# Second expert stage: the matrix engine's jump ahead of the first gather, seven zero products less

## What is computed

```python
probs_g = softmax(xf @ w_group + b_group);  p_top, g_idx = top_k(probs_g, 1)
in_group = (xf @ w_router + b_router) of group g_idx
w_top, e_local = top_k(softmax(in_group), 2);  w_top = w_top / sum(w_top)
gates = one_hot(g_idx * 4 + e_local) weighted by p_top * w_top
h = silu(einsum('td,edf->tef', xf, w_gate)) * einsum('td,edf->tef', xf, w_up)
y = einsum('tef,efd->td', h * gates[:, :, None], w_down)
```

## Time and profile before

| what | value |
|---|---|
| median of three runs (lowest, highest) | 907.32 us (905.35, 909.91) |
| profiled execution: span from first to last instruction | 902.7 us |
| PE busy in the span | 881.5 us (98%) |
| VectorE, ScalarE, GpSimd busy | 502.8, 391.4, 35.2 us |
| bytes moved, mean rate | 205.78 MB, 228 GB/s |

### The profile page before, as it was taken

One profiled execution on the slowest core, in us unless ns is written; L12 is line 12 of the kernel. 1 busy time (PEld: TensorE's weight loads), 2 busy tenths in 40 slices (PEclk: granted clock), 3 DMA queues, 4 the chain that ended last, 5 costly groups with the idle time before them and its releaser, 6 DMA issues.

```text
span 902.7 us, 13442 instructions
## 1 busy us (share of the span) xinstructions
PE 881.5 (98%) x5387; PEld 678.2 (75%) x5387; DVE 502.8 (56%) x752; ACT 391.4 (43%) x531; POOL 35.2 (4%) x73
## 2 busy tenths in 40 slices
PE   7999999989999999999999999999999999999998
PEld 6988998944543698878545446899877888888887
DVE  4798876711111965626211118465658777777576
ACT  4755654232221536551322215435545666655441
POOL 7100010000000000000000000000001000000010
PEclk9999999999999999999999999999999999999999
DMA  9934417979999574329599996354543655546611
GB/s 319 318 96 139 141 47 263 341 254 411 409 409 401 179 242 169 100 89 351 190 411 409 409 403 216 122 181 166 176 152 118 219 192 192 187 139 233 234 47 46
DMA packets 102828, 205.78 MB, mean 228 GB/s; under 512 B 6896, under 2 KB 57840, under 8 KB 102768
## 3 DMA queue, kind: packets, MB, share of 16 engines
q1 hardware_dynamic: 101184, 202.14, 62.6%
q10 hardware_dynamic: 1584, 2.81, 1.0%
HBM read 203.87 MB, written 1.05 MB: 227 GB/s over the span
## 4 chain that ended last, share of the span: by engine, by line
PE 83%; DVE 5%; DMA 5%; ACT 4%; issue 2%; SPq 1%; DVEq 0%; ACTq 0%
PE psum L709 80%; DVE w_lo L2116 2%; DMA raw<-in_w_kv_shared 2%; ACT w_hi L1639 1%; DMA raw<-in_attn_w_in 1%; DMA raw<-in_a_w_in 1%; ACT arena L1639 1%; SPq L361 1%; PE psum L817 1%; DMA x_res<-in_x 1%; ACT x_slots L1639 0%; PE psum L1504 0%; PE psum L922 0%; DVE xt L2137 0%; PE psum L1018 0%
## 5 line engine op out<-in xcount | busy, mean ns | idle before, releaser
L709 PE MATMUL psum<-xt,w_hi 128*128 128x256 f32 (+1 forms) x1056 | 253.8, 321 | 3.9 <-DVEq L2831 1.7
L2116 DVE TENSOR_TENSOR w_lo<-raw,w_hi 128x2048 fp32r<-128x2048 f32 x88 | 200.7, 2287 | 47.4 <-ACT w_hi L1639 44.3
L709 PE MATMUL psum<-xt,w_lo 128*128 128x256 f32 x704 | 198.2, 282 | 0.0
L709 PEld LDWEIGHTS psum<-xt,w_hi 128*128 128x128 f32 x1056 | 177.1, 190 | 19.4 <-issue 2.7
L1639 ACT ACTIVATE w_hi<-raw 128x2048 fp32r<-128x2048 f32 (+1 forms) x90 | 170.1, 1892 | 38.8 <-PE psum L709 23.4
L709 PEld LDWEIGHTS psum<-xt,w_lo 128*128 128x128 f32 x704 | 134.1, 191 | 0.0
L709 PE MATMUL psum<-w_hi,xt 128*128 128x512 f32 (+1 forms) x368 | 112.8, 379 | 0.0
L1639 ACT ACTIVATE arena<-psum 128x512 f32<-128x512 f32 (+2 forms) x70 | 40.8, 601 | 124.9 <-PE psum L709 82.6
L709 PE MATMUL psum<-hi_as_raw,x_slots 128*64 128x512 f32 x176 | 80.8, 596 | 0.0
L709 PE MATMUL psum<-lo_as_raw,x_slots 128*64 128x512 f32 x176 | 80.8, 596 | 0.0
L709 PEld LDWEIGHTS psum<-w_hi,xt 128*128 128x128 f32 x368 | 67.3, 189 | 12.6 <-DVE xt L2137 1.1
(11 more groups left out here) (267 smaller groups left out, 1245.0 us busy)
## 6 DMA issues: line engine op xcount, KB each, us to landing
hi_as_raw<-in_gate_up SPq DMA_DIRECT2D x44, 512.0 KB, 7.7
lo_as_raw<-in_gate_up SPq DMA_DIRECT2D x44, 512.0 KB, 9.1
raw<-in_ffn_w_up SPq DMA_DIRECT2D x44, 512.0 KB, 4.5
raw<-in_gate_up SPq DMA_DIRECT2D x40, 512.0 KB, 6.8
raw<-in_a_w_in SPq DMA_DIRECT2D x26, 512.0 KB, 7.5
raw<-in_w_down SPq DMA_DIRECT2D x24, 512.0 KB, 10.5
raw<-in_attn_w_in SPq DMA_DIRECT2D x24, 512.0 KB, 5.0
raw<-in_ffn_w_down SPq DMA_DIRECT2D x22, 512.0 KB, 4.1
```

Source lines behind the costliest of these rows:

```text
L709: return pe.matmul(o, l, r, start=start, stop=stop, skip_group_check=skip)
L2116: return dve.tensor_tensor(w_half(h, w_lo), w_half(h, raw), w_half(h, w_hi).bitcast(F32), ALU.subtract).then_inc(lo_split, 1)
```

## The change

In stage 2 the seven zero products behind the count go. The first gather becomes a function. In stage 1 (`layer == 0`) it is called where it stood, ahead of the jump; in stage 2 it is called as the first thing in each of the two arms, so that the jump stands directly behind the register load.

```diff
                     keep_busy(8, 7)
                     count_chosen()
-                    keep_busy(7, 7)
                 pe.wait_ge(sem("placed"), layer + 1)
                 load = pe.value_load(load_max[0:1, 0:1], min_val=0, max_val=T)
...
-                pe.wait_ge(s["perm_ready"], 1)
-                for b in range(TB):
-                    pe.wait_ge(sem("x_rest"), 2 * layer + b + 1)
-                    for r, bank in enumerate(FIRST_BANKS):
-                        gather_block(0, r, bank, b)
+                def first_gather():
+
+                    pe.wait_ge(s["perm_ready"], 1)
+                    for b in range(TB):
+                        pe.wait_ge(sem("x_rest"), 2 * layer + b + 1)
+                        for r, bank in enumerate(FIRST_BANKS):
+                            gather_block(0, r, bank, b)
+
+                if layer == 0:
+                    first_gather()
                 with pe.If(load > FAST_LIMIT):
+                    if layer:
+                        first_gather()
                     dense_path()
                 with pe.Else():
+                    if layer:
+                        first_gather()
                     short_path()
```

## The result

The changed kernel takes 909.91 us (median of 18 runs, 906.95 to 915.37); the kernel before, run beside it, 905.46 (18 runs, 902.65 to 910.52). The ratio is 1.0044, with a 95% interval of 1.0029 to 1.0059: **4.0 us slower** by the ratio (the two medians lie 4.45 apart), where 0.3 us gained was forecast. The profiled execution of the changed kernel spans 906.1 us and took 907.79.

The account below looks back on a forecast made before the run. PE was taken to bound the kernel; the jump's visible 1.59 us would vanish but return ahead of the gather, so expert products start at 435.5 instead of 435.8, 0.3 gained: 907.0 us from 907.32, range 905.0 to 910.0.

Parts of the forecast that it names:

- What bounds the kernel, and the two gaps: PE bounds the kernel; at stage 2's head only its gaps of 0.64 and 1.59 us can be taken back.
- The price of the jump, 3.35: From PE's branch to the arm's first product takes 3.35 us, 1.8 of it hidden behind the gather in stage 2.
- one price fits both stages: The 3.35 us from stage 1's gap of 3.10 also gives stage 2's arm start, 435.7 against 435.80 measured.
- The register load, 0.25: The load that the moved jump needs at once in stage 2 costs 0.25 us, with up to 4.3 possible.
- The code packet under load, +0: Fetching the arm's code during stage 2's DMA traffic adds nothing, with up to 0.5 us in the range.
- Rival C, the clock: PE's 3.8 us of idle time ahead of stage 2's gather lowers the clock: 1.6 to 3.5 us lost, chance 0.30.
- The zero products, 0.45 gained: Without the seven zero products in stage 2, PE's instruction stream goes on at 428.05 instead of 428.5, 0.45 us gained.
- The expert products: In stage 2 they follow the gather without a jump, at 435.5 instead of 435.8, with the gates in time.
- The range: 905.0 to 910.0 us for the changed kernel, with C's slow end, the long load and scatter outside, under 0.2.
- my -0.3: The forecast's sum at stage 2's head: expert products 0.3 us earlier, 907.0 for the median.

Follow-up runs that it names:

- e8: The kernel before with PE's two arms in the other order in both stages, the short arm next in the code: 911.16 us, ratio 1.0066.
- e9: The kernel before with prefetch hints for PE's jump of both expert stages, both ahead of the router's products: 903.28 us, ratio 0.9979.
- e11: The kernel before with prefetch hints for both jumps, stage 1's earlier, ahead of the second half of projection O0: 904.8 us, ratio 0.9990.
- e12: The kernel before with 12 zero products between the first gather and the jump, in both stages: 909.14 us, one time.
- e4: The changed kernel without stage 2's register load on PE, its jump asking the register of stage 1: 909.29 us, ratio 1.0039.
- e5: The kernel before once more, unchanged, for a second trace: 907.02 us, one time.
- e2: The kernel before without the seven zero products, the jump where it was: ratio 0.9999.
- e1: The changed kernel with the seven zero products back behind the count, so the jump's move alone: ratio 1.0056 of the kernel before.
- e6: The changed kernel with 24 zero products in stage 2 between the register load and the jump: 909.68 us, ratio 1.0050.
- e7: The changed kernel with PE's two arms in the other order in both stages, the short arm first: 917.94 us, ratio 1.0141.
- e10: The changed kernel with prefetch hints for both jumps, stage 1's ahead of the second half of projection O0: 904.72 us, 0.9995 of the kernel before.
- e3: The kernel before with the register load moved behind the gather, directly ahead of the jump, in both stages: ratio 1.0032, 2.9 us.

## Why the prediction was wrong

- **What bounds the kernel, and the two gaps**: right. The gap of 1.59 was the jump (e8, e9 and e11 take it away), and the jump comes back ahead of the gather.
- **The price of the jump, 3.35**: this is the step that failed. I let the stream follow the gather at 0.12 for each product, set the branch at its end, 180.95 and 432.35, and counted the price from there. In fact the stream is well ahead of the gather: the code packet comes at least 0.8 (changed kernel) and 1.9 us (e12) before the last weight load ahead of stage 1's jump. With nothing queued the price is 5.45 (e4), and the gather hid 3.4 to 3.9 of it (5.45 less the gaps of 2.07 and 1.59), not 1.8. Where the stream stands is known only roughly: from the gather's start to the expert products of stage 2 it is 5.65 in the first trace of before and 6.13 in e5, which at a price of 5.45 puts the jump 0.2 to 0.7 after that start, but 7.13 in e2, whose gather ran at the lower clock. Why it varies is open. That "one price fits both stages" was no test, because stage 1's 3.10 was that execution's (e5); the row that spoke against me stood in my own text, stage 2's packet 0.5 to 0.7 *before* the gather's last load, and I put it down to the wait for x. The Trainium skill (TensorE: Matmul & The Clock Gate, Architectural detail) gives TensorE's queue as 64 deep; the gather is 32 weight loads and 32 products, and e12 and the changed kernel's stage 1 agree with a stream that far ahead.
- **The register load, 0.25**: mis-sized, 1.4 (e4 against the changed kernel and e1, each one trace). It lay between my bounds, 0 and 4.3; I took the middle of 0 and 0.45, because both rows were of this very load. The 0 was no bound, since a stream that runs ahead passes the load while PE works on what is queued (stage 1's maximum is ready at 175.03, 2.2 before the gather). In e6 PE's first product behind the load starts 0.71 after M, so the load holds up the stream by no more than that, and the jump waits for the rest. Before, it ran beside the wait for x.
- **The code packet under load, +0**: open. I took stage 1's jump for one without traffic, but the 0.04 of the earlier trace rows begins at 181.2, and in the 3 us before it, where a stream that runs ahead meets the jump, the same trace has transfers (columns as in the earlier trace rows):

```profile
178.00:179.00 1.00, 1.00 (x10) 1.00 (x10) 0.43 (x3) 0.02 (x1) 0.00 (x0) 1.00 1.01 320
179.00:180.00 1.00, 1.00 (x11) 1.00 (x10) 0.00 (x0) 0.18 (x1) 0.00 (x0) 1.00 0.46 148
```

e4's 5.45 was measured under traffic too (share 1.04). No trace shows a far jump that was surely taken without transfers, so how much of the 5.45 is theirs is not shown.
- **Rival C, the clock**: right in kind, with its place ahead of the gather; 0.30 was too little, since the idle time came out at 7.13, not 3.8, and e2 shows a fall within 2.35. Its price, 5.51 - 4.05 = 1.5, is below my 1.9 to 3.8, since PE stood idle in the first half of the stretch at the lower clock; the 2.0 to 2.7 of e4, e7 and e10 lie within. The granted clock of the 18 runs is 0.9938 in the mean and 0.996 at most; of 31 runs of the kernel before it was 0.9986, with 10 at 1.000.
- **The zero products, 0.45 gained**: not seen (e2, where the packet came later after M and not earlier).
- **The expert products** did follow the gather, and the gates were in time, as forecast.
- **The range**: 909.91 lies inside 905.0 to 910.0, but that is luck. The jump's price, the largest term, stands in none of its cases, and the kernel before came out at 905.46 beside it, 1.9 below the 907.32 on which the range was built.

The sum with the measured terms: my -0.3, and 2.1 more for the jump, 1.2 more for the load, 1.5 for the clock, make +4.5. The trace says 4.6 against the first trace of before and 4.1 against the second, the runs 4.0 (2.6 to 5.3).

## What to carry to other kernels

A jump to code that lies far away has a full price, here 5.45 us on TensorE (one trace, with transfers running), and its visible gap is only what the work queued ahead of it leaves over. Before moving such a jump to where the engine has nothing queued, find out how much was hidden: compare the start of the work ahead (not its end) with the arm's first instruction, in more than one trace. If the gap must go, fetch the target ahead or let the likely arm stand next in the code, and then look at the jump at the arm's other end. Here the first won the loss back without a measured gain over the kernel before, and the second lost more at that other end than it won.

## What the runs showed of the hardware that was not expected

- Code packets come 2.5 to 3.0 ahead of the arm's first product in nearly all traces (3.55 in e3's stage 1); the rest of the 5.45 lies ahead of the packet. The Trainium skill (Runtime: NRT & Kernel Launch, Instruction fetch mechanics) says that a taken branch whose target is not in the current window of two pages forces a fetch of that page before execution can go on; e8 (arm next in the code, no gap) and e11 (packet early, no gap) agree.
- The clock falls after quite different idle times: in e2, e7 and e10 it had fallen within a wait of 2.35, in e3 within stage 1's gap of 3.10, in e5 only behind stage 1's gap of 2.20, and in the first trace of before the same 3.10 left it at 1.00. Zero products helped only where they filled the wait itself (e6), not ahead of it (e1).
- e9 and e11 lose a visible 1.6 to 2.1 of stage 2's head but gain only 2.2 and 0.4 in the median. Both traces have the clock at 0.50 for 3.4 us from about 295 on, which the first trace of before has not; e4's trace has it too, without a hint, so it is not the hint's doing, but what it is was not tried.
